# 32 bytes of room behind each tile of the activations in a two-block transformer kernel

## The reference

```
h = h + 0.5 * swiglu(rmsnorm(h, ffn1_norm[l]), w_gate, w_up, w_down)   # 1024 -> 2816 -> 1024
u = rmsnorm(h, mix_norm[l])
z = u @ w_in[l]                                                       # projections of three mixers and their gates
...
h = h + merged @ w_out[l]
h = h + 0.5 * swiglu(rmsnorm(h, ffn2_norm[l]), ...)
```

## The kernel before, in words

| tensor | start before | phase before | phase after |
|---|---|---|---|
| `w_high`, `w_low` (all three buffers) | 41088, 65664 | 128 | 128 |
| `x` | 98432 | 128 in all 8 tiles | 128, 160, 192, 224, 0, 32, 64, 96 |
| `ffn_hid`, `ffn_hid_high`, `ffn_hid_low` | 144032, 144032, 148128 | 160 | 160 |
| `mix_y_*`, `mix_pool_*` | 201248 to 221728 | 32 | 32 |
| `odd_o_high`, `odd_o_low` | 208928, 217120 | 32 | 32 |
| `even_ob_high`, `even_ob_low` | 183296, 179200 | 0 | 0 |

## Time and profile before

### The profile page before, as it was taken

The page is one execution under the profiler, slowest core; times in us unless marked ns, Lnnn a source line. Parts: engine busy times, 40 slices in busy tenths (PEclk is TensorE's granted clock), DMA queues, the critical chain, the costliest instruction groups (busy, mean ns, idle before and its releaser), DMA issues.

```text
span 1495.1 us, 23262 instructions
## 1 busy us (share of the span) xinstructions
PE 1486.9 (99%) x9780; PEld 1330.5 (89%) x9780; DVE 1164.3 (78%) x1538; ACT 792.7 (53%) x991; POOL 39.4 (3%) x41
## 2 busy tenths in 40 slices
PE   9999999999999999999999999999999999999999
PEld 8888898888988888888889878799999999989989
DVE  7987776687798875988758677879998899776744
ACT  6444455565454444544435466455545745775653
POOL 0000001210000000000001020000000000000000
PEclk9999999999999999999999999999999999999999
DMA  7555545444455545555554544455554453335531
GB/s 286 200 195 197 173 170 180 161 142 168 157 194 195 187 179 197 190 184 192 188 198 139 186 154 157 153 208 205 196 197 171 164 181 137 141 106 190 179 132 57
DMA packets 38967, 261.15 MB, mean 175 GB/s; under 512 B 4688, under 2 KB 5584, under 8 KB 9168
## 3 DMA queue, kind: packets, MB, share of 16 engines
q1 hardware_dynamic: 38000, 258.62, 49.2%
q10 hardware_dynamic: 864, 1.05, 0.2%
HBM read 258.61 MB, written 1.05 MB: 174 GB/s over the span
## 4 chain that ended last, share of the span: by engine, by line
PE 95%; DVE 3%; ACT 1%; DMA 0%; issue 0%; ACTq 0%
PE ps L275 20%; PE ps L212 15%; PE ps L214 14%; PE ps L213 14%; PE ps L282 11%; PE ps L761 8%; PE ps L763 4%; PE ps L300 1%; DVE w_low L202 1%; PE ps L1502 1%; PE ps L302 1%; PE ps L1493 0%; DMA w_raw<-in_weights 0%; PE ps L2355 0%; PE ps L1475 0%; ACT w_high L195 0%
## 5 line engine op out<-in xcount | busy, mean ns | idle before, releaser
L202 DVE TENSOR_TENSOR w_low<-w_raw,w_high 128x2048 fp32r<-128x2048 f32 (+2 forms) x244 | 551.6, 2262 | 148.1 <-ACT w_high L195 146.4
L195 ACT ACTIVATE w_high<-w_raw 128x2048 fp32r<-128x2048 f32 (+2 forms) x244 | 459.6, 1885 | 384.5 <-PE ps L282 171.2
L275 PE MATMUL ps<-x,w_high 128*128 128x512 f32 x1328 | 317.1, 391 | 0.0
L275 PEld LDWEIGHTS ps<-x,w_high 128*128 128x128 f32 x1328 | 243.9, 188 | 47.5
L761 PE MATMUL ps<-ffn_hid,w_high 128*128 128x512 f32 x528 | 183.2, 390 | 0.0
L282 PEld LDWEIGHTS ps<-x,w_low 128*128 128x128 f32 x1328 | 170.3, 191 | 6.4
L282 PE MATMUL ps<-x,w_low 128*128 128x256 f32 x1328 | 173.0, 283 | 0.0
L212 PE MATMUL ps<-w_high,x 128*128 128x512 f32 (+1 forms) x416 | 152.8, 367 | 0.0
L212 PE MATMUL ps<-x,w_high 128*128 128x256 f32 x520 | 150.2, 289 | 0.2 <-DVE x L338 0.2
L763 PE MATMUL ps<-ffn_hid,w_low 128*128 128x256 f32 x528 | 148.9, 282 | 0.0
L214 PE MATMUL ps<-w_high,x 128*128 128x512 f32 (+1 forms) x416 | 148.8, 358 | 0.0
(11 more groups left out here) (471 smaller groups left out, 2329.8 us busy)
## 6 DMA issues: line engine op xcount, KB each, us to landing
w_raw<-in_weights SPq DMA_DIRECT2D x231, 1024.0 KB, 4.8
w_raw<-in_weights SPq DMA_DIRECT2D x10, 768.0 KB, 4.5
w_raw<-in_weights SPq DMA_DIRECT2D x5, 512.0 KB, 3.9
even_second_vectors<-in_second SPq DMA_DIRECT2D x1, 1836.0 KB, 7.4
resid<-in_x SPq DMA_DIRECT2D x3, 256.0 KB, 6.0
w_raw<-in_weights ACTq DMA_DIRECT2D x3, 256.0 KB, 7.7
out<-resid SPq DMA_DIRECT2D x3, 256.0 KB, 2.3
table<-in_table SPq DMA_DIRECT2D x1, 737.0 KB, 7.5
```

What stands on the lines that cost most here:

```text
L195: act.activation(self.wh[:, j, 0:SIZES[n]], self.raw[:, j, 0:SIZES[n]], ACT.Copy).then_inc(self.hi_made, 1)
L202: dve.tensor_tensor(self.wl[:, j, 0:SIZES[n]], self.raw[:, j, 0:SIZES[n]], self.wh[:, j, 0:SIZES[n]].bitcast(F32), ALU.subtract).then_inc( ...
L275: pe.matmul(c.bank(bank + i).rearrange("p (a t) -> p a t", a=2), wh[:, k, i * P:(i + 1) * P], c.x[:, :, k, :], start=(k == 0), stop=False, ...
```

## The change

One line: the last axis of `x` is allocated with 8 more float32 (32 bytes), and all code goes on with the first 256. So tile k starts 1056*k bytes behind the part's start instead of 1024*k, and the low part starts 8448 bytes behind the high part (33 times 256), so the two runs of one 512-column matmul have the same phase as each other. `x` grows by 512 bytes for each partition; every tensor behind it moves up by 512 bytes and keeps its phase. Instructions, their order on each of the five engines, and their waits are the same.

```diff
-        self.x = sb("x", [P, 2, DT, SEQ], F32R)
+        self.x = sb("x", [P, 2, DT, SEQ + 8], F32R)[:, :, :, 0:SEQ]
         self.xh, self.xl = self.x[:, 0], self.x[:, 1]
```

## The result

The changed kernel takes 1500.83 us (median of 20 runs, 1500.04 to 1502.38) against 1497.99 for the kernel before (20 runs beside it), 2.8 us more; the ratio of the runs is 1.0024, 95% interval 1.0017 to 1.003. It is slower, by just more than the 0.2% that the prediction took as the limit of what can be told. The profiled execution took 1501.85 us, its span is 1500.1 us.

A forecast was written before the change was run, and what follows sets the result against it. It took PE's matmuls to bound the kernel: -6.6 + 2.7 + 3.0 - 0.6 = -1.5 us against the profiled 1496.88, carried over to the median 1498.22 as 1496.7 us; range of 8 in 10: 1490 to 1503.5.

The forecast's parts named there:

- What bounds the kernel: PE, busy 99% of the span; its gain or loss per matmul comes out at the end nearly one for one.
- The mechanism: `x` placed off the weights' phase: 256-column matmuls save 1 to 5 ns, 512-column ones lose or stay.
- no-effect rival: Moving tiles by 32 bytes changes nothing, tensors differ for other reasons: 1498.2 us; chance 0.10.
- B: L275, `x` moving with 512 columns, 1328 matmuls: +2 ns each, +2.7 us; ends -1.3 and +6.6.
- C: L212 to L214, `x` stationary, 512 columns of weights moving, 864 matmuls: +3.5 ns each, +3.0 us.
- the jump of the phase: At L275 the moving operand's phase changes after every two matmuls; reason to put its cost above L761's.
- A: L282 and L212 to L214, `x` moving with 256 columns, 2888 matmuls: -2.3 ns each, -6.6 us.
- only every second tile gains: Weak end for 256 columns of `x` moving, made possible by `even_ob`'s 282: -1.3 ns each, -3.8 us.
- D: L212 to L214, `x` stationary, 256 columns of weights moving, 384 matmuls: -1.5 ns each, -0.6 us.
- At nothing: L300 and L302 under 0.3 us; dearer ACT and DVE writes of `x` under PE; other tensors keep their phase.
- slower rival: L275 pays 396, C becomes +4.3 us: sum +3.7, 1501.9 us, or 1504.7 with A weak; chance 0.16.

The follow-up runs named there:

- together32: Against the kernel before, the split weights, `x` and everything behind moved up 32 bytes together, so phase differences stay; 1497.67 against 1497.41 us.
- weights160: Against the kernel before, only the split weights moved, to phase 160, `x` staying at 128; 1505.38 us, ratio 1.0056.
- all160: Against the kernel before, all eight tiles of `x` put at phase 160, that of `ffn_hid`; 1499.71 us, ratio 1.0016.
- all0: Against the kernel before, all eight tiles of `x` put at phase 0, 128 bytes from the weights' phase; 1503.45 us, ratio 1.0041.
- low96: Against the kernel before, only the low weights `w_low` moved, to phase 96; 1499.19 against 1497.64 us, ratio 1.001.
- low160: Against the kernel before, only the low weights `w_low` moved, to phase 160; 1498.19 us, ratio 1.0006.
- shift512: Against the kernel before, 512 bytes added behind `x` as a whole, so only the tensors behind it moved; 1497.54 against 1497.54 us.
- low_first: Against the kernel before, the low part of `x` put first at phase 128, the high part behind it at 160; 1495.09 against 1497.41 us.

## Why the prediction was wrong

**What bounds the kernel**: right for most of the time. Of the 3.8 us that the trace adds after the start, 3.0 are distances of PE's matmuls. But not everything that PE gains comes out "nearly one for one", and DVE does not always lie under PE though it is idle 22% of the span: at L2369 PE waits away the 0.8 us that it had gained in that stage. No term of the sum stood for such a wait.

**The mechanism**: right in that place alone changes the distance, with one sign for 256 columns and the other for 512, and that the loads beside the former go from 191 to 188 ns. The no-effect rival is out: together32 against weights160 shows that the difference of the phases does it. Why a shorter load and a longer distance go with these phases is not shown.

The Trainium skill's "SBUF — State Buffer", section "Who interferes with whom", gives the matrix engine independent read ports for moving operand and weight loads and lets it wait for no one; by that the change would have come to zero. weights160, where of the operands of L275 only the weights lie elsewhere, is 0.56% slower, so the measurement decides against it here. The Trainium skill's "TensorE: Matmul & The Clock Gate", section "LDWEIGHTS", has a load of 128 columns take 128/1.2 = 107 ns, which 213 ns of columns would hide; by that estimate B and C would have stayed at zero. The trace disagrees: its loads for L275 take 188 ns, which 213 would hide too, and B is at +5.0 us, C at +3.6.

**B, the step that failed.** I took +2 ns for L275, "nearer to L761, because it too has the moving operand displaced", and away from the 393 to 396 of the earlier trace rows, because there the stationary one is. Which operand is displaced is not what matters: L275 pays 395 with `x` moved (all160) and 396 with the weights moved (weights160). And L761's 390 was no evidence that displacement is free: in weights160, without displacement, it takes 392. L761 alternates with 256-column matmuls, L275 and the rows follow others of their length; that was the likeness to go by. L300 and L302, which alternate on the very operands of L275 and L282, bear this out at the phase that `ffn_hid` has: in all160, behind the start (48 matmuls each), L300 goes from 231.4 to 229.0 ns and L302 from 115.6 to 118.2, the pair from 347.1 to 347.2, while L275 with the same tensors at the same phases rises by 4.9. At other phases this pair rises too (350.8 in all0). B measured +3.8 ns, +5.0 us, against +2.7. The reason for staying above L761, the jump of the phase, was wrong too, since all160 has none and pays more.

**A, the second step that failed**: right in sign, too large. -1.5 ns for L282 and -1.9 for L212 to L214, together -5.0 us, where I had -6.6; within my ends. I read a difference of mean durations as one of distance, and in the earlier trace rows that does not hold to a ns: in the kernel before, the distances of the same six rows are 118.5, 119.4, 115.8, 118.8, 117.0 and 119.7, a mean of 118.2 against 119.7 for `x`, so 1.5 less and not 2.7. Nor was place all that told them apart: the three `ffn_hid` rows come together at 116.7 to 116.9 once `x` alone has moved. And the mean of the earlier trace rows stood mostly for the phases 160 and 32; all0 shows that phase 0 gives 0.9 ns where 160 gives 2.9, and the changed kernel goes through all eight. My end for "only every second tile gains", -3.8, was the better reading of `even_ob_low`'s 282.

**C** came to +3.6 us where I had +3.0; its rows were the right ones, and the discount for one tile at its old phase was too much. **D** is -0.6, as predicted, which was luck: no row had its form, and I had taken the middle between two ends. **At nothing**: L300 and L302 at +0.2 are; of the lines of `exact3` without `x`, which were to stay, those with `ffn_hid` gave -0.6 and those with `mix_y` and `odd_o` +0.4; and the wait for DVE gave +0.8.

So B and A together are 3.9 us off (2.3 and 1.6), C 0.6, the other way the 0.6 of `ffn_hid`; with the 0.2 of L300 and L302 that leads from -1.5 to +2.6, and with the 0.4 and the 0.8 to the +3.8 of the trace. The slower rival had the mechanism, rows for L275; it decided at 394, below the 396 where I had put its point, because that point was worked out with A at its full size. That its sum, +3.7 us, is nearly the trace's is luck: it had B and C too dear, A's gain too large, and no wait. I had written that the prediction fails if L275 leaves 390 to 395; it failed with L275 at 394, inside that band, because a band of 5 ns over 1328 matmuls is 6.6 us, wider than the question.

## What to carry to other kernels

When a row of the same kernel is borrowed for an operation that it doesn't have, choose it by what runs before and after it (alone in its form, or alternating with another) before choosing it by which operand differs. Where thousands of equal matmuls bound a kernel, measure distances from start to start to a tenth of a ns: 1 ns in a rounded mean of L275 was 1.3 us here, a third of what the change cost; and a difference of durations is not one of distances. Placement by the difference of phases can be tried part by part, since the forms want opposite things: displacing only the half of `x` that the 256-column pass reads, and reading it last in the 512-column matmul, gave -1.7 us in the trace (-2.3 in the medians) where displacing all gave +3.8 (+2.8). A gain on the bounding engine is worth its sum only as far as no other engine is next in line: here 0.8 us went into one wait.

## What the runs showed of the hardware that was not expected

- Where two operands lie is worth some 2% of a matmul, with opposite signs: L275 (512 columns) runs 228.4 ns apart with `x` and all weights at one phase, 229.1 and 229.8 with the low weights alone elsewhere, and 230.2 to 233.3 wherever `x` or its own weights lie elsewhere; L282 (256 columns) 119.5 at one phase and 116.6 to 118.6 at others.
- The load that runs beside a matmul counts: the last L275 of a slot, beside which the first low weights are loaded, goes from 226.6 to 235.0 ns when only `w_low` lies at another phase, 32 bytes below or above that of `x` (low96, low160).
- A line can change though none of its own operands does: the `ffn_hid` lines of `exact3` went from 117.9 to 116.8 ns in the changed kernel with none of their own operands at a new phase, and stayed at 117.9 in shift512. In low_first L213 gained 2 ns although the part of `x` that it reads stayed at the weights' phase. That its neighbours do this is likely, but not shown.
- Within a slot of the kernel before, the first five distances of L275 are on average 233.4, 234.7, 229.0, 232.5 and 230.3 ns before they settle at 226.6 to 227.4: with equal phases, too, a sequence takes some five matmuls to find its pace.
- A wait of PE of 1.5 us at the start left the clock at 1.00 in the kernel before; one of 2.33 us was followed by 3.2 us at 0.51 (the 1.2 GHz level) in the changed one. Ten matmuls of L300 and L302 that took 2.0 us in the former (from 12.5 us on) took 3.2 in the latter (from 12.8 us on).
